# Weights times values in the MLA heads: the outer and the inner queries side by side in the two column halves of TensorE

## The reference, cut to what matters

```python
def mla_attend(q_lat, q_rope, c_kv, k_rope, q_pos, k_pos):
    s = (einsum('bqhc,bkc->bhqk', q_lat, c_kv) + einsum('bqhr,bkr->bhqk', q_rope, k_rope)) * ATTN_SCALE
    mask = k_pos[None, :] <= q_pos[:, None]
    p = softmax(where(mask, s, -inf), axis=-1)
    return einsum('bhqk,bkc->bqhc', p, c_kv)

def mla_output(o_lat, w_uv, w_o):
    v = einsum('blhc,chv->blhv', o_lat, w_uv).reshape(B, L, N_HEADS * V_HEAD)
    return v @ w_o
```

## Time and profile before

| | us |
|---|---|
| median of 3 runs | 1513.22 (1513.07 to 1514.79) |
| the profiled execution, device time | 1515.17 |
| span of that execution, first to last instruction | 1513.2 |
| PE busy in it | 1445.9 (96%) |
| DVE, ACT, POOL busy | 689.2, 527.0, 233.8 |
| granted TensorE clock, mean | 0.983 |

### The profile page before, as it was taken

One profiled execution on the slowest core, in us unless ns is written; L12 is line 12 of the kernel. 1 busy time (PEld: TensorE's weight loads), 2 busy tenths in 40 slices (PEclk: granted clock), 3 DMA queues, 4 the chain that ended last, 5 costly groups with the idle time before them and its releaser, 6 DMA issues.

```text
span 1513.2 us, 26366 instructions
## 1 busy us (share of the span) xinstructions
PE 1445.9 (96%) x10332; PEld 1310.8 (87%) x10332; DVE 689.2 (46%) x958; ACT 527.0 (35%) x841; POOL 233.8 (15%) x327
## 2 busy tenths in 40 slices
PE   9999999997898999999999999999899999999997
PEld 9756666554688999999999989999799999999996
DVE  4535555532258323222322576887833332233355
ACT  4135454432234322112222247882432211222224
POOL 0020000100056000000000345234620000000034
PEclk9999999998999999999999999999999999999999
DMA  7230000023121333312233222222122331223301
GB/s 203 68 88 19 16 12 22 0 64 103 45 84 57 87 91 98 101 56 84 83 94 115 63 63 63 67 79 88 56 84 83 104 105 55 84 83 94 115 1 59
DMA packets 180547, 111.09 MB, mean 73 GB/s; under 512 B 25608, under 2 KB 178781, under 8 KB 180480
## 3 DMA queue, kind: packets, MB, share of 16 engines
q1 hardware_dynamic: 179888, 109.37, 24.8%
q0 software_dynamic: 592, 0.79, 0.2%
HBM read 107.11 MB, written 3.02 MB: 73 GB/s over the span
## 4 chain that ended last, share of the span: by engine, by line
PE 83%; DVE 8%; ACT 4%; POOL 2%; issue 2%; SPq 1%; DMA 0%; DVEq 0%; ACTq 0%; POOLq 0%
PE ps L495 53%; PE ps L549 6%; PE ps L773 3%; PE ps L720 3%; PE ps L734 3%; DVE xT L1668 2%; PE ps L754 2%; DVE wl L1396 1%; PE ps L688 1%; ACT wh L1080 1%; PE ps L858 1%; PE ps L841 1%; PE ps L885 1%; PE ps L628 1%; DVE xl L1674 1%
## 5 line engine op out<-in xcount | busy, mean ns | idle before, releaser
L495 PE MATMUL ps<-xh,wl 128*128 128x280 f32 x1584 | 334.7, 292 | 0.0
L495 PE MATMUL ps<-xh,wh 128*128 128x280 f32 x1584 | 333.3, 292 | 0.6 <-DVE wl L1396 0.5
L495 PE MATMUL ps<-xl,wh 128*128 128x280 f32 x1584 | 331.7, 291 | 0.0
L495 PEld LDWEIGHTS ps<-xh,wh 128*128 128x128 f32 x1584 | 252.5, 189 | 1.6 <-issue 1.0
L495 PEld LDWEIGHTS ps<-xh,wl 128*128 128x128 f32 x1584 | 252.9, 189 | 0.0
L495 PEld LDWEIGHTS ps<-xl,wh 128*128 128x128 f32 x1584 | 250.3, 188 | 0.0
L1396 DVE TENSOR_TENSOR wl<-raw,wh 128x2048 fp32r<-128x2048 f32 (+2 forms) x79 | 198.0, 2507 | 99.7 <-ACT wh L1080 99.7
L1080 ACT ACTIVATE wh<-raw 128x2048 fp32r<-128x2048 f32 (+2 forms) x79 | 162.9, 2061 | 204.0 <-PE ps L495 190.8
L1714 DVE TENSOR_TENSOR ht<-sg,ps 128x560 f32<-128x560 f32 x44 | 32.5, 738 | 273.1 <-PE ps L495 264.1
L1311 ACT ACTIVATE hh<-ht 128x560 f32 (+1 forms) x44 | 29.6, 672 | 271.6 <-DVE ht L1714 271.6
L1898 POOL TENSOR_TENSOR acc<-xT 128x560 f32<-128x560 f32 x4 | 5.6, 1399 | 726.2 <-DVE xT L1611 669.3
(11 more groups left out here) (306 smaller groups left out, 2373.3 us busy)
## 6 DMA issues: line engine op xcount, KB each, us to landing
raw<-in_ffn_w_gu SPq DMA_DIRECT2D x176, 256.0 KB, 3.6
raw<-in_ffn_w_down SPq DMA_DIRECT2D x48, 384.0 KB, 4.3
raw<-in_lru_w_in SPq DMA_DIRECT2D x16, 512.0 KB, 4.5
Ctok<-in_cache_latent SPq DMA_DIRECT2D x48, 128.0 KB, 2.0
raw<-in_mla_w_o SPq DMA_DIRECT2D x16, 256.0 KB, 3.7
raw<-in_ffn_w_down SPq DMA_DIRECT2D x16, 256.0 KB, 5.1
raw<-in_lru_w_o SPq DMA_DIRECT2D x16, 256.0 KB, 3.3
raw<-in_mla_w_in SPq DMA_DIRECT2D x9, 256.0 KB, 5.4
```

The source lines that it names most:

```text
L495: mm = pe.matmul(ps[:, 1024 * jp + 512 * h:1024 * jp + 512 * h + TH], w[:, k, col:col + P], x[:, k, h * TH:(h + 1) * TH], start=(k == 0 an ...
```

## The change

The queries are cut differently: into four quarters of 132 (`QG`). The outer half is the first and the last quarter, the inner half the two in the middle. Both now go to bank 6 alone, outer on partitions 0 to 63, inner on partitions 64 to 127, whatever the head is. The matmuls of the two halves are written alternately where they can be, ten in all. The columns of the outer half are 264, 4, 132, 132, 132 and 16, of the inner half 264, 264, 140 and 12: 680 each. ACT reads the product in two instructions of 264 columns, and DVE in two, each from its own 64 partitions; both halves still end on the head's own rows of `xh` and `xl`. `o_sum` and `o_hi` now count two for a head.

```diff
+QG = NP // 4
...
+        def queries_of(inner):
+
+            return ps[64 * inner:64 * inner + 64, 3072:3072 + 2 * QG].rearrange("p (a c) -> p a c", a=2)
...
-                hp = NP // 2
-                for j in range(5):
-                    kk = P if j < 4 else META
-                    for half in range(2):
-                        q0 = max(P * j, half * hp)
-                        q1 = (half + 1) * hp
-                        if q0 >= q1:
-                            continue
-                        at = 512 * (6 + half) + q0 - half * hp
-                        mm = pe.matmul(ps[64 * u:64 * u + VH, at:at + q1 - q0], Vs[u][0:kk, j, :],
-                                       PT[:, j, q0:q1] if j < 4 else PT4[:],
-                                       start=(j == 0), stop=(j == 4 or (half == 0 and j == 2)))
-                mm.then_inc(o_sum, 1)
+                outer, inner = ps[0:VH, 3072:3072 + NP // 2], ps[64:64 + VH, 3072:3072 + NP // 2]
+                v = [Vs[u][0:(P if j < 4 else META), j, :] for j in range(5)]
+                ends = PT[:, 0, :].rearrange("p (g c) -> p g c", g=4)[:, 0:4:3, :]
+                pe.matmul(outer, v[0], ends, start=True, stop=False)
+                pe.matmul(inner, v[0], PT[:, 0, QG:3 * QG], start=True, stop=False)
+                pe.matmul(outer[:, P:QG], v[1], PT[:, 1, P:QG], start=False, stop=False)
+                pe.matmul(outer[:, QG:2 * QG], v[1], PT[:, 1, 3 * QG:NP], start=False, stop=False)
+                pe.matmul(inner, v[1], PT[:, 1, QG:3 * QG], start=False, stop=False)
+                pe.matmul(outer[:, QG:2 * QG], v[2], PT[:, 2, 3 * QG:NP], start=False, stop=False)
+                pe.matmul(inner[:, 2 * P - QG:2 * QG], v[2], PT[:, 2, 2 * P:3 * QG], start=False, stop=False)
+                pe.matmul(outer[:, QG:2 * QG], v[3], PT[:, 3, 3 * QG:NP], start=False, stop=False)
+                pe.matmul(inner[:, 3 * P - QG:2 * QG], v[3], PT[:, 3, 3 * P:3 * QG], start=False, stop=True).then_inc(o_sum, 1)
+                pe.matmul(outer[:, 2 * QG - META:2 * QG], v[4], PT4[:], start=False, stop=True).then_inc(o_sum, 1)
...
-                act.wait_ge(o_sum, h + 1)
-                dst = xh[64 * u:64 * u + 64, bass.ds(p, 1), 0:NP].rearrange("p a (h c) -> p (a h) c", h=2)
-                act.activation(dst, pair(3, 64 * u, 64 * u + 64)[:, :, 0:NP // 2], ACT.Copy).then_inc(o_hi, 1)
+                act.wait_ge(o_sum, h * 2 + 2)
+                dst = xh[64 * u:64 * u + 64, bass.ds(p, 1), 0:NP].rearrange("p a (g c) -> p (a g) c", g=4)
+                act.activation(dst[:, 0:4:3, :], queries_of(0), ACT.Copy).then_inc(o_hi, 1)
+                act.activation(dst[:, 1:3, :], queries_of(1), ACT.Copy).then_inc(o_hi, 1)
...
-                dve.wait_ge(o_hi, h + 1)
...
+                dve.wait_ge(o_hi, h * 2 + 1)
+                dve.tensor_tensor(dst[:, 0:4:3, :], queries_of(0), hi[:, 0:4:3, :], ALU.subtract)
+                dve.wait_ge(o_hi, h * 2 + 2)
+                dve.tensor_tensor(dst[:, 1:3, :], queries_of(1), hi[:, 1:3, :], ALU.subtract).then_inc(o_lo, 1)
```

More of the change, by code:

```diff
@@ L423, in _ @@
             sp.wait_ge(ql_sum, HEADS)
-            sp.wait_ge(o_sum, HEADS)
+            sp.wait_ge(o_sum, 2 * HEADS)
             sp.wait_ge(s_lout[0], 96)
@@ L1514, in outputs_lo @@
             def outputs_lo(h, p, u):
-                dve.wait_ge(o_hi, h + 1)
                 rows = slice(64 * u, 64 * u + 64)
[L1518 to L1521, removed]
+                dst = xl[rows, bass.ds(p, 1), 0:NP].rearrange("p a (g c) -> p (a g) c", g=4)
+                hi = xh[rows, bass.ds(p, 1), 0:NP].rearrange("p a (g c) -> p (a g) c", g=4).bitcast(F32)
+                dve.wait_ge(o_hi, h * 2 + 1)
+                dve.tensor_tensor(dst[:, 0:4:3, :], queries_of(0), hi[:, 0:4:3, :], ALU.subtract)
+                dve.wait_ge(o_hi, h * 2 + 2)
+                dve.tensor_tensor(dst[:, 1:3, :], queries_of(1), hi[:, 1:3, :], ALU.subtract).then_inc(o_lo, 1)
             def head(p, u):
@@ L1876, in _ @@
                     swap(u)
-                    pool.wait_ge(o_sum, i * 2 + (u + 1))
+                    pool.wait_ge(o_sum, i * 4 + (2 * u + 2))
                     values(i * 2 + (u + 2), u)
```

## The result

The changed kernel takes 1497.96 us (median of 4 runs, 1496.37 to 1498.63) against 1513.43 for the kernel before beside it: ratio 0.9895, 95% interval 0.9879 to 0.9911. It is 1.05% faster; forecast were 1497.1 us and a range of 1493 to 1502. The profiled execution took 1498.63 with a span of 1496.8, 16.4 us less than the span of 1513.2 before.

The account below looks back on a forecast made before the run. PE was taken to bound the heads. Terms of -17.6 (blocks), +1.0 (keys), +0.7 (even heads), +0.3 (tail) and -0.5 (clock) sum to -16.1 us, from 1513.22 to 1497.1 us; range 1493 to 1502.

Parts of the forecast that it names:

- PE is the bound in the heads: Over some thirteen heads PE works 176.4 of 179.3 us, so time cut from its block of outputs shortens the whole.
- The price of a column, 0.833 ns, and two halves at once: Block of outputs on PE: overlapping column halves cut it from 2.74 to 1.64 us; 16 blocks give -17.6 us.
- The halves draw their records independently: PE's block of outputs: each column half draws its own records ahead, so unequal pieces do not stall the halves.
- the rival in program order: PE's block: each matmul waits for the start of the one written before; saves 0.88 us a block, 1500.6 us; chance 0.10.
- The give-back: Longer ACT and DVE reads behind the block cost PE +1.0 us at keys, +0.7 in even heads, +0.3 in the tail.
- same columns in two instructions, +0.16: ACT's and DVE's reads of the product: splitting each into two instructions of 264 columns adds 0.16 us on either engine.
- The keys' term: Keys (L711) in six heads already wait for `xl`, so the later read counts fully: 6 x 0.16 = +1.0 us.
- The last but one block at the lower clock: At half the clock the streaming removed there is worth 2.2 us instead of 1.1; half the difference taken, -0.5 us.
- Sum: All terms together: -16.1 us, from 1513.22 to 1497.1 us.
- the 2 us of range kept for this: Where the other low-clock stretches fall will shift: no term, only 2 us of range either way.
- rival 2: Behind the block, DVE's queries, PE's sequencer or second DVE instruction late in every head: 1500 to 1502 us; chance 0.12.

Follow-up runs that it names:

- outer-first version: Changed kernel with the five 128-row outer pieces written first, then the four inner ones, then the 16-row outer piece: 1513.12 us, ratio 0.9990.
- padded version: Changed kernel with the product's last piece (16 keys) zero-padded to 128 rows: 1497.72 us, ratio 0.9880; run again 1496.77 us, ratio 0.9874.

## Why the prediction was right, point by point

- *PE is the bound in the heads, and a block's saving is a saving of the whole.* Right. One half instead of two gives all of it back.
- *The price of a column, 0.833 ns, and two halves at once.* Right: 1.61 us instead of the 1.64 forecast, a saving of 1.12 (forecast 1.10). 16 x 1.12 = 17.9.
- *The halves draw their records independently.* Right for this order, and the rival in program order (1.85 us) wrong. The limit that I had only guarded against ("over such a distance") is real: in the outer-first version the inner half passed three records that had not started, and stood idle while there were four. The rule of the Trainium skill (TensorE: Matmul & The Clock Gate, "Part 3: Packing small matmuls") that matmuls start strictly in program order does not hold for the two column halves here: L776 starts at 189.58 us, ahead of L775 at 189.66, which stands before it in the program.
- *The give-back.* Its places were right, but for one that was missed: the last head, which makes no keys, lost 0.12 like an even one (its period went from 11.66 to 10.66 with a block shorter by 1.12). The keys gave back 6 x 0.10 = 0.6 us (forecast 1.0), the even heads 7 x 0.12 = 0.8 (forecast 0.7). Its cause, "same columns in two instructions, +0.16", failed: two instructions on the same partitions cost 0.06 us at ACT and nothing in the period, since they overlap; changing partitions between them costs the overlap. That the size came out near was luck: without the overlap, and only so, two instructions take what the fixed cost gives (DVE 0.87 us as forecast, ACT 0.80 for 0.76). The keys' term was too large because DVE also starts its first half 0.07 us sooner behind its row maximum, which I had left out. From DVE's rows of 705 and 191 ns I had taken a fixed cost per instruction that sits one behind the other; they can't show that, and the pair at L1179 would have shown that a change of partitions matters.
- *The last but one block at the lower clock, -0.5 us beyond its share.* It went from 4.41 us, start to start, to 2.65: -1.76, forecast -1.6. What followed it took 0.33 us more, where 0.16 were forecast.
- *Sum.* From the first block to the first fill the traces differ by 16.65 us; my terms for that stretch give 16.2. Behind the heads the difference moves to 17.5 (the sample's part, and a third of a microsecond before the heads), and falls by 1.0 to the end. That last step is no larger than what two traces of the changed kernel differ by: from L957 of before to the end it is 1103.7 us in the trace of before, and for the changed kernel 1104.8 in the first trace and 1103.1 in the second, with 30.9 and 24.1 us at the lower clock (29.7 in the trace of before). The median missed the forecast by 0.9 us, well within the 2 us of range kept for this.
- *Sequencer and queries (rival 2).* Not here; L1518 ends in time at a block of 1.61 us. At 1.46 it seems not to: the padded version shows 1.55 ahead of even heads. The margin was as narrow as it looked.

## What to carry to other kernels

If a matmul has at most 64 output rows and another with the same contraction is independent of it, give them different halves of the output partitions and write them alternately, no more than two float32 matmuls of one half ahead of the other's; the price of a pair can be read from any place of the trace that does so already. Ask next what the halves do to those who read them, and what has become free: here a PSUM bank, which was worth another 5 us, a third of the change itself. To price a split instruction, look at whether two like instructions in a row, on the partitions that yours will use, overlap in the trace, not at a fixed cost from a line through two sizes.

## What the runs showed of the hardware that I had not expected

- A column half started a record past three records of the other half that stood ahead of it and had not started (128.77 in the outer-first version, 189.58 in the changed kernel), and in the outer-first version stood idle while there were four or more.
- ACT and DVE started an instruction up to 0.1 us before the end of the one before when both started on the same partition (ACT 0.66 us for two of 0.38, DVE 0.76), and 0.01 to 0.02 us behind it when the partition changed (0.80 and 0.87 us).
- A wait of 0.55 us on PE cost 0.79 us of period: the gap shown leaves out the overlap of matmuls that it breaks.
- A stretch at the lower clock of 1.2 GHz at the end of the heads had 0, 3.4 or 13.7 us in the traces. Runs of one and the same kernel differ in their clock: the eight of the padded version had a mean clock of 0.978 to 0.981 or of 0.984 to 0.985, and the first four were 3.4 us longer on average. One trace can't stand for a kernel's median here. The changed kernel and the padded one, 2.2 us apart by the periods of their heads, had medians 0.2 us apart in one comparison and 1.9 in the other.
